# Residual kept by tokens; output and down projections with activations stationary and 512 weight columns moving

## The chip, the cores and the metric

The kernel runs on one core of one Trainium2 chip. The metric is the device time of one execution in microseconds; the figure given for a kernel is the median of several runs. Inputs are fp32 in HBM, and the output is fp32.

## What is computed

One layer on 256 tokens of width 2048. With `rmsnorm(u, w) = u * rsqrt(mean(u*u) + EPS) * w`, the reference is, cut to what matters:

```
h = rmsnorm(x, mix_norm_w);  u = h @ w_in                      # 2048 -> 5664
y_fox = fox_attention(...);  y_ssd = ssd_mixer(...)            # from slices of u
x = x + concat([y_fox, y_ssd]) @ w_out                         # 2048 x 2048
h = rmsnorm(x, ffn_norm_w)
g, up = split(h @ w_gate_up);  g = causal_dwconv(g, ...)       # 2048 -> 2 x 5632
x = x + (silu(g) * up) @ w_down                                # 5632 x 2048
h = rmsnorm(x, ple_norm_w)
x = x + sigmoid(h @ w_ple_gate) * (p @ w_ple_proj)
return rmsnorm(x, final_norm_w)
```

## The kernel before, in words

Every product is made of three TensorE products of rounded parts: a value is split into a high part (`hi`, type fp32r) and the rest (`lo`), and hi·hi, hi·lo and lo·hi are summed in PSUM. Weights stream from HBM in chunks of 256 rows by 512 columns (512 KB) through a ring of four slots: SyncE issues the load (`load_chunk`, two issues a chunk in the FFN), ScalarE makes `w_hi` (`make_hi`, L312), VectorE makes `w_lo` (`make_lo`, L317), and TensorE multiplies. ScalarE may make the high part of chunk n+4 only when TensorE is done with chunk n. All engines walk the chunks in the same order, and their other work is hung between chunks by hand: a step that belongs to the end of a group of chunks stands on ScalarE and VectorE `LEAD` = 3 chunks behind that end, since these engines run ahead of TensorE by that much. `plan()` fills the tables of such steps for the first part of the program.

The stages, in order: 11 groups of 8 chunks of `w_in` with the attention and the SSD part between them; `w_out` (4 groups `o0` to `o3` of 8 chunks); the FFN (22 units of 8 chunks, in a loop of two units); the down projection (4 groups of 22 chunks, partly in a loop on TensorE); the tail (per-layer gate `pg0` to `pg3`, 8 chunks each, with one chunk `pp0` to `pp3` of the projection of p after the sixth); the final norm and eight stores.

There are three forms of the product of one chunk, all with 6144 moving columns in sum:

- `multiply` (L332 to L334): a 128x128 tile of weights is stationary and 256 tokens move; 24 matmuls a chunk. Used in `w_in` (but for v) and in `w_out`.
- `multiply_wide` (L344, L346): a tile of weights is stationary; the high and low part of the activations, 512 columns, move past `w_hi`, and 256 columns past `w_lo`; 16 matmuls a chunk. Used in the FFN and the down projection.
- by tokens (L372 to L374, in `multiply_group`): a 128x128 tile of activations is stationary and 512 weight columns move; 12 matmuls a chunk. Used for v and in the tail.

The first two leave results with channels on partitions, the third with tokens on partitions. The residual is `xT`, with channels on partitions. It is made at the start by turning x (`turn_x`, L679) and copying each pair of turned tiles out of PSUM on VectorE (`copy_x`, L1538). After each group of `w_out` VectorE adds the result to it (`add_to_residual`, L1250; for the down projection `add_down`, L1262, four adds a group), ScalarE and VectorE make the parts of the next h from it (`make_h`, L969 and L1243), and GpSimd sums its squares (L646 to L653). `stats` on TensorE sums these over partitions (L713 before the second FFN unit, L716 in the tail). In the tail TensorE turns the residual back, eight 128x128 tiles for each of four groups (`turn_residual`, L936), and ScalarE copies it to `out_tok`. The last group of the tail has its weights kept (`last_hi`, `last_lo`), so that the first 128 tokens can be finished before the others.

## Time and profile before

| | |
|---|---|
| median of 3 runs | 1260.08 us (1260.00 to 1260.17) |
| the profiled execution | 1260.43 us, its span in the trace 1258.7 us |
| mean granted TensorE clock, share of full speed | 0.998 |
| TensorE busy | 1245.7 us, 99% of the span |
| VectorE, ScalarE, GpSimd busy | 856.7, 616.9, 60.8 us |
| HBM read | 224.03 MB, 180 GB/s over the span |

The profiled execution is 0.35 us longer than the median. A matmul's row in the trace starts when it is issued and overlaps the next one, so what one costs is the distance between starts, not its duration. A few per cent of the matmul rows are missing from the trace, so distances are read over stretches where every row is there, or over whole stages with the count that the program gives.

### The profile page before, as it was taken

The numbers are of one execution on the slowest core, as the hardware profiler recorded it, in microseconds if no ns is written. First come the engines' busy times: TensorE is split into PE (matmuls) and PEld (weight loads), VectorE is DVE, ScalarE is ACT, GpSimd is POOL, SyncE is SP. The second block draws the span as 40 slices with busy tenths as digits, with TensorE's granted clock in tenths as the row PEclk, the third lists the DMA queues.
The fourth block names the chain that finished last, engine by engine and source line by source line (L and its number), as shares of the span: only waits on it lengthen the run. The fifth ranks groups of instructions, "written<-read, shape, count | busy, mean of one in ns | idle before, by whom it ended". The sixth has DMA issues, their size and how long they took to land.

```text
span 1258.7 us, 21432 instructions
## 1 busy us (share of the span) xinstructions
PE 1245.7 (99%) x7838; PEld 1108.7 (88%) x7838; DVE 856.7 (68%) x1120; ACT 616.9 (49%) x810; POOL 60.8 (5%) x66
## 2 busy tenths in 40 slices
PE   8999999999999999999999999999999999999997
PEld 7999998789999888888888888888888888888885
DVE  6698777677678776767767677676746464646554
ACT  6544555656444454444444454454444344444555
POOL 2000000001213100000000000000001010101000
PEclk9999999999999999999999999999999999999999
DMA  8566555344656666666666666666665656566652
GB/s 256 168 183 184 157 146 155 114 114 125 199 172 203 186 193 186 185 196 183 191 193 185 194 187 187 194 187 188 191 190 166 216 160 217 164 212 202 198 185 101
DMA packets 165885, 226.94 MB, mean 180 GB/s; under 512 B 10209, under 2 KB 101381, under 8 KB 165701
## 3 DMA queue, kind: packets, MB, share of 16 engines
q1 hardware_dynamic: 165732, 225.90, 59.3%
q8 instruction: 38, 0.62, 0.2%
q0 software_dynamic: 96, 0.26, 0.1%
q14 instruction: 19, 0.15, 0.0%
HBM read 224.03 MB, written 2.10 MB: 180 GB/s over the span
## 4 chain that ended last, share of the span: by engine, by line
PE 97%; DVE 1%; DMA 1%; ACT 0%; SPq 0%; issue 0%; ACTq 0%; DVEq 0%
PE ps L344 39%; PE ps L346 19%; PE ps L332 8%; PE ps L333 8%; PE ps L334 8%; PE ps L372 4%; PE ps L374 4%; PE ps L373 3%; DMA w_raw<-in_w_in 1%; PE ps L764 1%; PE ps L767 1%; PE ps L808 1%; DVE h_parts L1243 0%; PE ps L791 0%; PE ps L821 0%; PE ps L778 0%
## 5 line engine op out<-in xcount | busy, mean ns | idle before, releaser
L317 DVE TENSOR_TENSOR w_lo<-w_raw,w_hi 128x1024 fp32r<-128x1024 f32 x413 | 505.9, 1230 | 318.2 <-ACT w_hi L312 317.5
L312 ACT ACTIVATE w_hi<-w_raw 128x1024 fp32r<-128x1024 f32 x413 | 435.9, 1059 | 459.4 <-PE ps L346 341.2
L344 PE MATMUL ps<-h_parts,w_hi 128*128 128x512 f32 x1408 | 488.6, 394 | 0.0
L346 PE MATMUL ps<-h_parts,w_lo 128*128 128x256 f32 x1408 | 390.2, 277 | 0.0
L344 PEld LDWEIGHTS ps<-h_parts,w_hi 128*128 128x128 f32 x1408 | 264.0, 188 | 61.5
L346 PEld LDWEIGHTS ps<-h_parts,w_lo 128*128 128x128 f32 x1408 | 264.2, 188 | 0.0
L344 PE MATMUL ps<-act_parts,w_hi 128*128 (+1 forms) x704 | 244.4, 392 | 0.0
L346 PE MATMUL ps<-act_parts,w_lo 128*128 (+1 forms) x704 | 196.8, 280 | 0.0
L332 PE MATMUL ps<-h_parts,w_hi 128*128 128x256 f32 x576 | 165.8, 288 | 0.6 <-DVE w_lo L317 0.6
L333 PE MATMUL ps<-h_parts,w_hi 128*128 128x256 f32 x576 | 162.9, 283 | 0.0
L334 PE MATMUL ps<-h_parts,w_lo 128*128 128x256 f32 x576 | 162.9, 283 | 0.0
L344 PEld LDWEIGHTS ps<-act_parts,w_hi 128*128 128x128 f32 x704 | 132.1, 188 | 29.5 <-issue 0.4
L346 PEld LDWEIGHTS ps<-act_parts,w_lo 128*128 128x128 f32 x704 | 132.2, 188 | 0.0
L332 PEld LDWEIGHTS ps<-h_parts,w_hi 128*128 128x128 f32 x576 | 110.2, 191 | 1.4 <-issue 1.3
L333 PEld LDWEIGHTS ps<-h_parts,w_hi 128*128 128x128 f32 x576 | 110.4, 192 | 0.0
L334 PEld LDWEIGHTS ps<-h_parts,w_lo 128*128 128x128 f32 x576 | 110.2, 191 | 0.0
L332 PE MATMUL ps<-mixHi,w_hi 128*128 128x256 f32 x256 | 71.8, 280 | 0.0
L334 PE MATMUL ps<-mixHi,w_lo 128*128 128x256 f32 x256 | 71.6, 280 | 0.0
L333 PE MATMUL ps<-mixLo,w_hi 128*128 128x256 f32 x256 | 71.6, 280 | 0.0
L372 PE MATMUL ps<-w_hi,h_parts 128*128 128x512 f32 x168 | 67.0, 399 | 0.6 <-DVE w_lo L317 0.6
L374 PE MATMUL ps<-w_hi,h_parts 128*128 128x512 f32 x168 | 65.8, 392 | 0.0
L373 PE MATMUL ps<-w_lo,h_parts 128*128 128x512 f32 x168 | 65.4, 389 | 0.0
(248 smaller groups left out, 1115.3 us busy)
## 6 DMA issues: line engine op xcount, KB each, us to landing
w_raw<-in_w_gate_up SPq DMA_DIRECT2D x352, 256.0 KB, 3.2
w_raw<-in_w_in SPq DMA_DIRECT2D x88, 512.0 KB, 3.7
w_raw<-in_w_down SPq DMA_DIRECT2D x88, 512.0 KB, 4.6
w_raw<-in_w_out SPq DMA_DIRECT2D x32, 512.0 KB, 4.6
w_raw<-in_w_ple_gate SPq DMA_DIRECT2D x32, 512.0 KB, 4.6
w_raw<-in_w_ple_proj SPq DMA_DIRECT2D x4, 512.0 KB, 5.3
out_x<-out_tok SPq DMA_DIRECT2D x8, 256.0 KB, 2.9
xtok<-in_x SPq DMA_DIRECT2D x3, 512.0 KB, 9.1
```

The lines of the kernel that those rows point to most:

```text
L312: act.activation(parts(n)[0], w_raw[:, n % RING, :], ACT.Copy).then_inc(w_hi_made, 1)
L317: dve.tensor_tensor(lo, w_raw[:, n % RING, :], hi, ALU.subtract).then_inc(w_lo_made, 1)
L332: pe.matmul(dst, hi, opHi(k), start=start and m % 2 == 0, stop=False, skip_group_check=True)
L333: pe.matmul(dst, hi, opLo(k), start=False, stop=False, skip_group_check=True)
L334: mm = pe.matmul(dst, lo, opHi(k), start=False, stop=stop, skip_group_check=True)
L344: pe.matmul(ps[:, bank_of[m], :], hi, both.rearrange("p b t -> p (b t)"), start=first and k == 0, stop=False, skip_group_check=True)
L346: mm = pe.matmul(ps[:, bank_of[m], T:2 * T], lo, both[:, 0, :], start=False, stop=last and k == 1, skip_group_check=True)
L372: pe.matmul(dst, a, hi, start=first and kk == 0, stop=False)
L373: pe.matmul(dst, a, lo, start=False, stop=False)
L374: mm = pe.matmul(dst, b, hi, start=False, stop=last and kk == 1)
L764: pe.matmul(ps[:, bank, 0:3 * P], sel[0:both, j:j + 1].to_broadcast([both, P]), row[:, :], start=start, stop=False, skip_group_check=True)
L767: mm = pe.matmul(ps[:, bank, dst:dst + P], ident_bf[:, :], mask[:, :], start=False, stop=True, skip_group_check=True)
```

## The change

- The residual is `xtok`, tokens on partitions, for the whole kernel: x as it is loaded. `xT`, `copy_x`, `turn_residual`, `copy_residual` and `out_tok` are gone; the tail adds into `xtok` and the stores read it.
- `w_out` and the down projection use the third form. The down projection is written out on TensorE, without a loop; each group has banks of its own.
- After each of the eight groups VectorE adds two [128x512] results to `xtok` (`add_columns`), ScalarE squares these columns and sums along them (`square_columns`), and TensorE, two chunks after the group's end, turns the new columns (`turn_columns`, eight 128x128 tiles) into the group's own PSUM banks. ScalarE and VectorE make the parts of h from PSUM, five chunks after the group's end in their own order.
- The sums of squares are summed over groups on VectorE (`sum_columns`), ScalarE takes the root, and VectorE inverts it (`invert_root`). For the FFN, `spread_rms` turns the column into rows on TensorE, as was done for the first norm only, and VectorE copies it. GpSimd no longer sums the residual's squares.
- At the start, h is made from the turned tiles in PSUM, without a copy between.
- The arena in SBUF starts at a multiple of 64 bytes instead of 32. It holds `act_parts`, `mixHi`, `mixLo`, `last_hi` and `last_lo`; before, these started at 32 past such a multiple. `w_hi`, `w_lo` and `h_parts` lie outside it and start at a multiple of 64 in both.

```
+    OUT_SETS, DOWN_SETS = (SET_B, SET_A, SET_C, SET_D), (SET_C, SET_A, SET_B, SET_D)
+    out_groups = [Group(f"o{i}", wout_v, COLS * i, "mix", b, KP, by_token=True) for i, b in enumerate(OUT_SETS)]
...
-        xT = sb("xT", [P, KD, T])
+        xtok = sb("xtok", [P, TT, D])
...
-        arena = (nc.sbuf_base + 31) // 32 * 32
+        arena = (nc.sbuf_base + 63) // 64 * 64
...
-        evacuated |= {f"o{i}": (x_new, NORM + 2 * i + 2) for i in range(NDN)}
-        evacuated |= {f"dn{i}": (x_new, 2 * NORM + 2 * i + 2) for i in range(NDN)}
+        evacuated |= {f"o{i}": (h_lo_made, KD + MT * (i + 1)) for i in range(NDN)}
+        evacuated |= {f"dn{i}": (h_lo_made, 2 * KD + MT * (i + 1)) for i in range(NDN)}
...
+        TURN_AFTER = 2
...
                 after(act_after, end[g] + LEAD, "leave_out", i)
                 after(dve_after, end[g] + LEAD, "leave_out", i)
+                all_after(end[g] + TURN_AFTER, "turn_out", i)
...
+            def turn_columns(i, banks, new):
+
+                pe.wait_ge(x_new, new)
+                for m in range(MT):
+                    for t in range(TT):
+                        k = MT * i + m
+                        mm = pe.transpose(ps[:, banks[m // 2], m % 2 * T + t * P:m % 2 * T + (t + 1) * P],
+                                          xtok[:, t, k * P:(k + 1) * P], ident[:, :])
+                mm.then_inc(x_turned, 1)
...
+                    if j == 0 and k == TURN_AFTER - 1:
+                        turn_out(NDN - 1)
+                    if j == 0 and k == SPREAD1_AT:
                         pe.wait_ge(*evacuated["o0"])
-                        stats(1, 4, columns=False)
+                        spread_rms(1, OUT_SETS[0][0])
...
+                        dst = ps[:, DOWN_SETS[g][t], :]
+                        pe.matmul(dst, a, hi, start=first and kk == 0, stop=False)
+                        pe.matmul(dst, a, lo, start=False, stop=False)
+                        mm = pe.matmul(dst, b, hi, start=False, stop=last and kk == 1)
...
+                    chunk(j)
+                    if g > 0 and j == TURN_AFTER - 1:
+                        turn_down(g - 1)
...
-                if n == STATS2_AT:
-                    stats(2, GATE_BANKS[1][0], rows_=False)
-                if n % GROUP == XTURN_AT:
-                    turn_residual(i)
+                if n == TURN_AFTER - 1:
+                    turn_down(NDN - 1)
...
+            def square_columns(norm, i):
+                for t in range(TT):
+                    done_ = TT + NDN * TT * (norm - 1) + TT * i + t
+                    act.wait_ge(x_new, NDN * TT * (norm - 1) + TT * i + t + 1)
+                    act.wait_ge(x_squared, done_)
+                    act.activation(sq[:, :, :], xtok[:, t, i * COLS:(i + 1) * COLS], ACT.Square,
+                                   accum_out=x_ssq[:, norm - 1, t, i:i + 1]).then_inc(x_squared, 1)
...
-                dve.wait_ge(h_hi_made, norm * KD + k + 1)
-                dve.scalar_tensor_tensor(hLo[:, k, :], xT[:, k, :], gain[:, k:k + 1], hHi[:, k, :],
+                dve.wait_ge(h_hi_made, norm * KD + k // 2 * 2 + 2)
+                dve.scalar_tensor_tensor(hLo[:, k, :], turned_x(norm, k)[0], gain[:, k:k + 1], hHi[:, k, :],
...
+            def add_columns(i, banks):
+
+                for t in range(TT):
+                    cols = xtok[:, t, i * COLS:(i + 1) * COLS]
+                    dve.tensor_tensor(cols, ps[:, banks[t], :], cols, ALU.add).then_inc(x_new, 1)
```

On TensorE, the start of the down projection before: a weight tile is stationary (the second name), 512 and 256 columns of `act_parts` move in turn.

```order
L344 MATMUL ps<-act_parts,w_hi 128x512 [waits w_lo_made,ffn_lo,ffn_out]
L346 MATMUL ps<-act_parts,w_lo 128x256
L344 MATMUL ps<-act_parts,w_hi 128x512
L346 MATMUL ps<-act_parts,w_lo 128x256
L344 MATMUL ps<-act_parts,w_hi 128x512
L346 MATMUL ps<-act_parts,w_lo 128x256
```

The same engine after the change, at the end of the second chunk of the second group of the down projection, with the new turn of the first group's columns:

```order
L916 MATMUL ps<-w_lo,act_parts 128x512
L917 MATMUL ps<-w_hi,act_parts 128x512
L718 MATMUL ps<-ident,xtok 128x128 [waits x_new]
L718 MATMUL ps<-ident,xtok 128x128 x7
L915 MATMUL ps<-w_hi,act_parts 128x512 [waits w_lo_made]
L916 MATMUL ps<-w_lo,act_parts 128x512
L917 MATMUL ps<-w_hi,act_parts 128x512
```

Weights now move, 512 columns at a time, and eight turns stand behind a wait for VectorE's adds. On VectorE, the start of the tail before (the first row is the low parts of chunks 0 to 3):

```order
L317 TENSOR_TENSOR w_lo<-w_raw,w_hi 128x1024 [waits w_hi_made] x4
L1262 TENSOR_TENSOR xT<-ps,xT 128x512 [waits w_used]
L1262 TENSOR_TENSOR xT<-ps,xT 128x512
L1262 TENSOR_TENSOR xT<-ps,xT 128x512 [waits x_part] x2
L1243 SCALAR_TENSOR_TENSOR h_parts<-xT,par,h_parts 128x256 [waits h_hi_made] x4
L317 TENSOR_TENSOR w_lo<-w_raw,w_hi 128x1024 [waits w_hi_made] x6
```

And after the change, at the same place:

```order
L318 TENSOR_TENSOR w_lo<-w_raw,w_hi 128x1024 [waits w_hi_made] x4
L1251 TENSOR_TENSOR xtok<-ps,xtok 128x512 [waits w_used]
L1251 TENSOR_TENSOR xtok<-ps,xtok 128x512
L318 TENSOR_TENSOR w_lo<-w_raw,w_hi 128x1024 [waits w_hi_made]
L1255 TENSOR_REDUCE x_sum<-x_ssq 128x2 [waits x_squared]
L1259 RECIPROCAL rms_col<-root 128x2 [waits root_made]
L318 TENSOR_TENSOR w_lo<-w_raw,w_hi 128x1024 [waits w_hi_made]
L1244 SCALAR_TENSOR_TENSOR h_parts<-ps,par,h_parts 128x256 [waits h_hi_made] x4
```

The adds are two instead of four, and the four instructions that make h stand two chunks later, with two low parts between.

## Rows read from the trace of the kernel before

**Rows 1.** The page: busy time of each engine, the granted clock, the chain.

```profile
PE 1245.7 (99%) x7838; PEld 1108.7 (88%) x7838; DVE 856.7 (68%) x1120; ACT 616.9 (49%) x810; POOL 60.8 (5%) x66
...
PEclk9999999999999999999999999999999999999999
...
PE 97%; DVE 1%; DMA 1%; ACT 0%; SPq 0%; issue 0%; ACTq 0%; DVEq 0%
```

**Rows 2.** TensorE in time (start, duration, instruction): first and last of 105 in `w_out`.

```profile
349.75 0.28 PE L332 MATMUL ps<-mixHi,w_hi 128*128 128x256 f32 x1
...
361.95 0.28 PE L334 MATMUL ps<-mixHi,w_lo 128*128 128x256 f32 x1
```

**Rows 3.** TensorE in time: the first matmul of the down projection and the first after it.

```profile
901.21 0.39 PE L344 MATMUL ps<-act_parts,w_hi 128*128 128x512 f32 x1
...
1145.55 0.40 PE L372 MATMUL ps<-w_hi,h_parts 128*128 128x512 f32 x1
```

**Rows 4.** TensorE in time: ends of a run of 11 by tokens in v, of 107 in the tail.

```profile
196.54 0.39 PE L373 MATMUL ps<-w_lo,h_parts 128*128 128x512 f32 x1
...
198.84 0.39 PE L374 MATMUL ps<-w_hi,h_parts 128*128 128x512 f32 x1
...
1189.81 0.39 PE L373 MATMUL ps<-w_lo,pHi 128*128 128x512 f32 x1
...
1213.93 0.40 PE L374 MATMUL ps<-w_hi,h_parts 128*128 128x512 f32 x1
```

**Rows 5.** TensorE in time: first and last of 36 with the kept weights.

```profile
1238.15 0.40 PE L372 MATMUL ps<-last_hi,h_parts 128*128 128x512 f32 x1
...
1246.34 0.40 PE L374 MATMUL ps<-last_hi,h_parts 128*128 128x512 f32 x1
```

**Rows 6.** TensorE in time: the first turn of the tail, and the small sums.

```profile
1162.75 1.03 PE L936 MATMUL ps<-ident,xT 128*128 128x128 f32 x8
...
1163.85 0.40 PE L373 MATMUL ps<-w_lo,pHi 128*128 128x512 f32 x1
...
1169.16 0.50 PE L716 MATMUL ps<-ones,sumsq 128*128 128x1 f32 x4
...
1169.84 0.39 PE L373 MATMUL ps<-w_lo,h_parts 128*128 128x512 f32 x1
```

**Rows 7.** TensorE in time: the sum before the FFN's second unit, and the first norm's spread.

```profile
426.54 0.59 PE L713 MATMUL ps<-sumsq,ones 128*128 128x256 f32 x2
...
427.20 0.28 PE L346 MATMUL ps<-h_parts,w_lo 128*128 128x256 f32 x1
...
43.03 0.61 PE L725 MATMUL ps<-ident,rms_col 128*128 128x128 f32 x4
...
43.60 0.28 PE L333 MATMUL ps<-h_parts,w_hi 128*128 128x256 f32 x1
```

**Rows 8.** TensorE in time: before the fifth chunk of the tail.

```profile
1156.26 0.39 PE L374 MATMUL ps<-w_hi,h_parts 128*128 128x512 f32 x1
1157.21 0.47 PE L372 MATMUL ps<-w_hi,h_parts 128*128 128x512 f32 x1 [0.57 <-DVE w_lo L317]
1157.52 0.40 PE L373 MATMUL ps<-w_lo,h_parts 128*128 128x512 f32 x1
```

**Rows 9.** VectorE in time, from the end of the down projection.

```profile
1148.05 2.48 DVE L1262 TENSOR_TENSOR xT<-ps,xT 128x512 f32<-128x512 f32 x4
1150.50 4.88 DVE L1243 SCALAR_TENSOR_TENSOR h_parts<-xT,par,h_parts 128x256 fp32r<-128x256 f32 x4
1155.31 5.16 DVE L317 TENSOR_TENSOR w_lo<-w_raw,w_hi 128x1024 fp32r<-128x1024 f32 x4
```

**Rows 10.** The start: VectorE's first copy, TensorE's second turn and first product.

```profile
5.38 0.69 DVE L1538 COPY xT<-ps 128x512 f32<-128x512 f32 x1 [1.79 <-PE ps L679]
...
7.53 0.66 PE L679 MATMUL ps<-ident,xtok 128*128 128x128 f32 x4 [0.98 <-DMA xtok<-in_x]
...
9.44 0.36 PE L332 MATMUL ps<-h_parts,w_hi 128*128 128x256 f32 x1 [0.16 <-DVE w_lo L317]
```

More of the change, by code:

```diff
@@ L354, in build, with turned_x @@
         WIDE_BANKS = ((0, 1, 2, 3), (4, 5, 6, 7))
+        def turned_x(norm, k):
+            if norm == 0:
+                bank, turn = X_BANKS[(k // 2) % len(X_BANKS)], k // 2
+            else:
+                bank = (OUT_SETS, DOWN_SETS)[norm - 1][k // MT][k % MT // 2]
+                turn = KD // 2 + NDN * (norm - 1) + k // MT
+            return ps[:, bank, k % 2 * T:(k % 2 + 1) * T], turn + 1
         def multiply_group(pe, n, g, c, only=(0, 1), between=None):
@@ L650, in _ @@
+            pool.wait_ge(a_exp, 1)
+            select(fdc[:, 3:4], fdc[:, 3:4], ALU.is_ge, 1.0, -H, 1, 0, 1).then_inc(a_ready, 1)
+            for b in range(WT // 2):
+                pool.wait_ge(gated, b // 2 + 1)
+                pair = xsT[:, 2 * b:2 * b + 2, :]
+                if b > 0:
+                    linked()
+                link(pool.tensor_tensor(sq[:, :, :] if b > 0 else sumsq[:, :, :], pair, pair, ALU.mult))
+                if b > 0:
                     linked()
                     link(pool.tensor_tensor(sumsq[:, :, :], sumsq[:, :, :], sq[:, :, :], ALU.add))
-                linked()
@@ L903, in _ @@
                 n0 = n_down + g * KDN
-                def chunk(j, q, first=False, last=False):
-                    at_ = (lambda k: act_parts[:, 2 * j + k, :, :]) if isinstance(q, int) else \
-                        (lambda k: act_parts[:, bass.ds(q * (2 * RING) + (2 * j + k), 1), :, :].rearrange("p a b t -> p (a b) t"))
-                    return multiply_wide(pe, n0 + j, at_, WIDE_BANKS[g % 2], first, last, q)
-                if g < 2:
-                    pe.wait_ge(ffn_out, NU + g)
-                else:
-                    pe.wait_ge(*evacuated[f"dn{g - 2}"])
@@ L940, in _ @@
+                if g < 3:
+                    pe.wait_ge(ffn_out, NU + g // 2)
+                pe.wait_ge(ffn_lo, NU - 2 if g == 0 else NU)
+                for j in range(KDN):
+                    if g == 0 and j == KDN - RING:
+                        pe.wait_ge(ffn_lo, NU)
+                    chunk(j)
+                    if g > 0 and j == TURN_AFTER - 1:
+                        turn_down(g - 1)
             for n, (g, c) in enumerate(tail):
@@ L1173, in _ @@
                     elif c == LEAD:
-                        for k in range(MT * (g - 1), MT * g):
-                            make_h(2, k, par_ple)
+                        leave_down(g - 1)
+                    elif c == LEAD + TURN_AFTER:
+                        turn_down(g - 1)
                 with act.Fori(0, (KDN - peeled) // RING) as q:
@@ L1190, in ple_sigmoid @@
                                    scale=rms_col[:, t:t + 1]).then_inc(ple_sig, 1)
-            def copy_residual(i):
-                for t in range(TT):
-                    act.wait_ge(xtok_turned, TT * i + t + 1)
-                    copy(out_tok[:, t, i * COLS:(i + 1) * COLS], ps[:, XTOK_BANKS[t], :]).then_inc(xtok_copied, 1)
             def square(i, t):
@@ L1525, in leave_out, with turn_out, leave_down, turn_down @@
                 dve.wait_ge(w_used, done[f"o{i}"] + 1)
-                add_to_residual(1, i, out_groups[i].banks)
+                add_columns(i, OUT_SETS[i])
+            def turn_out(i):
                 for k in range(MT * i, MT * (i + 1)):
                     make_h(1, k, par_ffn)
+            def leave_down(g):
+                dve.wait_ge(w_used, n_down + (g + 1) * KDN)
+                add_columns(g, DOWN_SETS[g])
+            def turn_down(g):
+                for k in range(MT * g, MT * (g + 1)):
+                    make_h(2, k, par_ple)
             def turn_par():
```

264 lines of the change are left out of this document (102 added, 162 removed).

## The prediction

> **What bounds the kernel now.** I read the page first: TensorE is busy for 99% of the span, the chain that ended last runs 97% through it, and its granted clock is in every slice 0.9 or more of full speed, in the mean 0.998, so at the 2.4 GHz level [rows 1]. VectorE is busy 68% and ScalarE 49% [rows 1]. So the time is a sum of TensorE's work, and the reader should look for three things: how far apart the starts of two matmuls lie in each form, how many turns there are, and at which few places TensorE still waits. For that I read TensorE in order of time, in stretches in which every row is there.
>
> The distance between starts, per 512 moving columns, is this. In `w_out`, 105 matmuls of 256 columns start from 349.75 to 361.95: 104 steps in 12.20 us, 0.1173 us each, 0.2346 us per 512 columns [rows 2]. The down projection takes 1145.55 - 901.21 = 244.34 us for 88 chunks of 6144 columns, 1056 times 512: 0.2314 us [rows 3]. By tokens, with 512 weight columns moving, the tail shows 24.12 us in 106 steps, 0.2275 us, and the v groups 2.30 us in 10, 0.230 us [rows 4]. The same form with the kept weights `last_hi` and `last_lo` moving takes 8.19 us in 35 steps, 0.2340 us [rows 5].
>
> **The change part by part.**
>
> Output projection. 32 chunks of 12 x 512 columns are 384 steps of 512. Before, 384 x 0.2346 = 90.1 us. After, the form is that of the tail, with the same ring of weights moving; only the stationary tiles come from another buffer. The trace bounds the pace at 0.2275 below and at 0.2340 above. I take 0.228: the tail's value is from 106 steps and v's from 10 that stand beside SSD work, so the tail is the nearer row. Gain: 384 x (0.2346 - 0.228) = 2.5 us.
>
> Down projection. 1056 x 0.228 = 240.8 us against 244.3: gain 3.6 us. The column count is the same, and no loop is left on TensorE; `w_out` is written out already and its matmuls start 0.117 us apart [rows 2], half the distance that is wanted here, so I cost the missing loop at nothing.
>
> Turns. Eight turns of eight tiles come in, four go out. The first one of the tail costs 1163.85 - 1162.75 = 1.10 us up to the second matmul behind it, of which 0.23 us is the matmul between: 0.87 us [rows 6]. Four more: +3.5 us. All of it is on the path, since TensorE has no idle time to put it in. A turn of the new kind differs in its buffers only; I know no row that would make it cheaper or dearer, and keep 0.8 to 1.0 us as its bounds.
>
> Small sums. The tail's sum over partitions, 1169.84 - 1169.16 = 0.68 us less one matmul of 0.23, goes: -0.45 us [rows 6]. The one before the second FFN unit (0.66 - 0.23 = 0.43 us) is replaced by a spread like that of the first norm (0.57 - 0.12 = 0.45 us): nothing [rows 7].
>
> The wait in the tail. At the fifth chunk TensorE is 1157.52 - 1156.26 = 1.26 us over two steps of 0.23: 0.80 us lost, 0.57 of it shown as a wait for `w_lo` [rows 8]. The cause stands on VectorE: four adds (2.48 us) and four parts of h (4.88 us) in one piece before the next low part, which begins at 1155.31 [rows 9]. After the change two adds (1.24 us) stand there, and the parts of h two chunks later. The next low part then can be ready long before 1156.5, so the 0.80 us go. What is late next? VectorE's adds end at 1148.05 + 1.24 = 1149.3. ScalarE's two squares, which no row shows at this place, are bounded by the dearest row of half that size, 1.22 us each [rows 9]: 1151.7. The high and the low part of chunk 4 at 1.29 us each, the low part's distance [rows 9]: 1154.3. TensorE wants it after four chunks and a turn, at 1145.55 + 4 x 2.74 + 0.87 = 1157.4. Nothing waits.
>
> The new wait. Each turn waits for the two adds, and all of TensorE's stream is queued behind it. TensorE gets there two chunks after the group's end, 1145.55 + 5.47 = 1151.0 in the tail's case; the adds end at 1149.3 [rows 3, 9]. The margin is 1.7 us, so I cost the eight waits at nothing.
>
> The kept weights. They start at 32 bytes past a multiple of 64 in SBUF, as does all of the arena, and are the only moving weights that do; they are also the only ones at 0.2340 [rows 5]. If that is the reason, 84 steps (36 for each half of the tokens and 12 of p) fall to 0.228: -0.5 us. The bounds are 0 and 0.55. I take 0.5, since same form and same stationary buffer leave little else.
>
> The start. The copy of 0.69 us goes from the chain to the first product [rows 10]. But TensorE itself gets its second turn only at 7.53, when x has landed, and runs filler until shortly before 9.44, where it waits only 0.16 us for the low part [rows 10]. Gain 0.2 us; the ends are 0 and 0.7.
>
> The squares that GpSimd did, the 16 copies and the rest on ScalarE and VectorE cost nothing: both engines have a third of the span free or more and run ahead of TensorE by up to four chunks.
>
> The sum: -2.5 - 3.6 + 3.5 - 0.45 - 0.8 - 0.5 - 0.2 = -4.6 us. It is made against the profiled execution, 1260.43 us, of which 1258.7 is the span: 1255.85. The median of the runs is 0.35 lower, so I predict 1255.5 us.
>
> One rule is to be weighed here. What the rows show is that 512 columns cost 14 ns more than 512 cycles at 2.4 GHz (213.3 ns), and 256 columns 10.6 ns more than theirs [rows 2, 4]. The Trainium skill, "TensorE: Matmul & The Clock Gate", section "Back-to-back issue gap", gives N / 2.4 + 2.5 ns. By it the new form would save only 12 x 2.5 ns on each of 32 chunks and 4 x 2.5 ns on each of 88, together 1.8 us instead of 6.1, and the time would be near 1259.8. The trace does not agree with the 2.5 ns in any form.
>
> **The rivals.**
>
> The pace belongs to the stage, not to the form. In the tail VectorE and ScalarE do less than beside v, where the same form runs at 0.230 [rows 4]. If `w_out` and the down projection run at 0.230, the gains shrink by 1440 x 0.002 = 2.9 us: 1258.4 us. For it: the v rows. Against it: those are 10 steps against 106, and neither `w_out` nor the down projection has matmuls of another kind in between, as v has. The page's rule would end close to this case.
>
> Slower: the new pair of operands is as slow as the kept weights, 0.2340, for instance because stationary and moving buffers disturb each other in a way that the tail's pair does not. Then `w_out` gains 0.2 us, the down projection loses 1056 x 0.2340 - 244.3 = 2.8 us, nothing comes from the kept weights, and the turns are not paid for: -0.2 + 2.8 + 3.5 - 0.45 - 0.8 - 0.2 = +4.6, so 1264.7 us. The point from which the change loses is a pace of (334.4 - 1.5) / 1440 = 0.2312 us, where 334.4 is the two stages now and 1.5 the sum of the other terms. Against it: both runs of by-token rows with the ring's weights are below that.
>
> Slower by waits: the adds come over 1.7 us later than I reckon, because VectorE is behind when a group ends. At 1 us lost in each of eight turns: 1263.5 us. Against it: VectorE's idle third.
>
> **How the numbers follow.** The forecast has 0.71, with a range of its own of 1254.0 to 1257.5 (paces of 0.2275 to 0.2293, the start's 0.7). The slower-stage case has 0.18, the pace of 0.2340 0.06, the waits 0.03; 0.02 are left for a larger gain. A measurement of this kernel can tell 0.2%, 2.5 us, from no change. So: faster 0.73, within 0.2% 0.18, slower 0.09. The range takes in the forecast and the first rival: 1252.8 to 1260.2 us.
>
> **What would show it.** In the trace of the changed kernel: steps of 0.228 us in both projections, the down projection in 240 to 241 us without its turns and `w_out` 2.5 us shorter; eight turns of 0.87 us with no idle time before them; no wait in the first chunks of the tail; the kept weights at 0.228; the first product at 9.3. The prediction is wrong if the steps are at 0.230 or more, if the turns wait, or if a low part is late after a group's end. TensorE's busy share stays at 99% in every case.

## The result, and the profile after

The changed kernel takes 1262.26 us, the median of 20 runs (1261.83 to 1262.71). The kernel before took 1260.01 us beside it (20 runs, 1259.77 to 1262.66). The ratio is 1.0016, with a 95% interval from 1.0009 to 1.0023. So the change costs some 2 us, where a gain of 4.6 was forecast; the time lies outside the range. The profiled execution took 1262.27 us, and its span is 1260.5 us, 1.8 us more than before.

The page of the changed kernel, in the same lines as [rows 1]:

```profile
PE 1248.1 (99%) x7132; PEld 1081.4 (86%) x7132; DVE 821.5 (65%) x1107; ACT 622.0 (49%) x834; POOL 23.2 (2%) x34
...
PEclk9999999999999999999999999999999999999999
...
PE 98%; DMA 1%; SPq 0%; ACT 0%; issue 0%; DVE 0%; ACTq 0%; DVEq 0%
```

TensorE issues 706 matmuls fewer than before and is busy 2.4 us longer. Its clock is as high as before. The groups of instructions of the page show where (line, engine, operation, tiles, shapes, count; then busy time and mean ns of one). First before, then after:

```profile
L344 PE MATMUL ps<-h_parts,w_hi 128*128 128x512 f32 x1408 | 488.6, 394 | 0.0
L346 PE MATMUL ps<-h_parts,w_lo 128*128 128x256 f32 x1408 | 390.2, 277 | 0.0
```

```profile
L345 PE MATMUL ps<-h_parts,w_hi 128*128 128x512 f32 x1408 | 497.6, 399 | 0.0
L347 PE MATMUL ps<-h_parts,w_lo 128*128 128x256 f32 x1408 | 395.4, 281 | 0.0
```

These are the FFN's matmuls. The change left them alone: the same instructions, the same number, the same buffers. Their busy times are up by 9.0 and 5.2 us (the rows of the two groups overlap in time, so the two numbers don't add up). To see what each stage did, I take the distance from the first matmul of a stage to the first of the next, in us. The front is from the first product to the output projection, and the tail is to the last matmul.

| | first product at | front | output | FFN | down | tail | span |
|---|---|---|---|---|---|---|---|
| before | 9.44 | 312.42 | 90.55 | 488.80 | 244.34 | 103.54 | 1258.7 |
| after | 8.82 | 311.86 | 90.27 | 498.65 | 242.11 | 99.21 | 1260.5 |
| difference | -0.62 | -0.56 | -0.28 | +9.85 | -2.23 | -4.33 | +1.8 |

Outside the FFN the stages lost 8.0 us together, three turns more in the output projection and three in the down projection already paid. The FFN, which the prediction costed at one turn, takes 9.85 us more. When the FFN became slow is seen in TensorE in time (start, duration, instruction, count), around its second unit:

```profile
416.59 1.03 PE L718 MATMUL ps<-ident,xtok 128*128 128x128 f32 x8
417.38 0.48 PE L345 MATMUL ps<-h_parts,w_hi 128*128 128x512 f32 x1
417.70 0.28 PE L347 MATMUL ps<-h_parts,w_lo 128*128 128x256 f32 x1
...
425.68 0.28 PE L347 MATMUL ps<-h_parts,w_lo 128*128 128x256 f32 x1
425.79 0.61 PE L704 MATMUL ps<-ident,rms_col 128*128 128x128 f32 x4
426.16 0.48 PE L345 MATMUL ps<-h_parts,w_hi 128*128 128x512 f32 x1
426.47 0.28 PE L347 MATMUL ps<-h_parts,w_lo 128*128 128x256 f32 x1
```

From 417.70 to 425.68 lie 46 steps of a half pair: 7.98 / 23 = 0.347 us for a pair (a matmul of 512 and one of 256 columns), 832 cycles at 2.4 GHz. Then come the small matmuls of `spread_rms`: two of 128 columns, which stand as x4, since a matmul of plain fp32 operands leaves two rows in the trace. Behind them a pair costs more, here between 599.72 and 619.86, 57 pairs in 20.14 us:

```profile
599.72 0.40 PE L345 MATMUL ps<-h_parts,w_hi 128*128 128x512 f32 x1
...
619.86 0.40 PE L345 MATMUL ps<-h_parts,w_hi 128*128 128x512 f32 x1
```

That is 0.3533 us, 848 cycles. It stays so up to 909.48: 2734 recorded steps at 424.0 cycles each. Nothing waits meanwhile. The kernel before shows both paces too. In its first FFN unit 29 pairs take 10.24 us, 0.3531 each; after its small matmul (L713, at 426.54 in [rows 7]) 59 pairs take 20.46 us, 0.3468 each:

```profile
415.93 0.40 PE L344 MATMUL ps<-h_parts,w_hi 128*128 128x512 f32 x1
...
426.17 0.40 PE L344 MATMUL ps<-h_parts,w_hi 128*128 128x512 f32 x1
...
599.26 0.40 PE L344 MATMUL ps<-h_parts,w_hi 128*128 128x512 f32 x1
...
619.72 0.39 PE L344 MATMUL ps<-h_parts,w_hi 128*128 128x512 f32 x1
```

So the same stream of matmuls runs at one of two paces, and it changes from one to the other at a few small matmuls. The kernel before runs 40 of its 1408 pairs at the slow pace, the changed one 16 and then 1368. The 1344 pairs more, at 16 cycles each, are 9.0 us.

### The profile page after: what moved, and what is told of

Read it like the earlier page. It is cut to its first block, busy times and chain, and to the rows that moved or that the text cites. A ratio compares the mean times of both kernels' runs of the same rounds, so it can differ in the third digit from the quotient of the medians.

```text
span 1260.5 us, 19756 instructions
## 1 busy us (share of the span) xinstructions
PE 1248.1 (99%) x7132; PEld 1081.4 (86%) x7132; DVE 821.5 (65%) x1107; ACT 622.0 (49%) x834; POOL 23.2 (2%) x34
## 4 chain that ended last, share of the span: by engine, by line
PE 98%; DMA 1%; SPq 0%; ACT 0%; issue 0%; DVE 0%; ACTq 0%; DVEq 0%
PE ps L345 26%; PE ps L347 13%; PE ps L916 6%; PE ps L915 6%; PE ps L917 6%; PE ps L382 6%; PE ps L384 6%; PE ps L383 6%; PE ps L333 5%; PE ps L335 5%; PE ps L334 5%; PE ps L763 1%; DMA w_raw<-in_w_in 1%; PE ps L718 1%; PE ps L766 1%; PE ps L807 1%
## 5 line engine op out<-in xcount | busy, mean ns | idle before, releaser
L345 PE MATMUL ps<-h_parts,w_hi 128*128 128x512 f32 x1408 | 497.6, 399 | 0.0
L915 PE MATMUL ps<-w_hi,act_parts 128*128 128x512 f32 x352 | 137.2, 390 | 0.0
L917 PE MATMUL ps<-w_hi,act_parts 128*128 128x512 f32 x352 | 137.0, 389 | 0.0
L916 PE MATMUL ps<-w_lo,act_parts 128*128 128x512 f32 x352 | 136.9, 389 | 0.0
L917 PEld LDWEIGHTS ps<-w_hi,act_parts 128*128 128x128 f32 x352 | 66.1, 188 | 13.8
L915 PEld LDWEIGHTS ps<-w_hi,act_parts 128*128 128x128 f32 x352 | 66.1, 188 | 13.7
L916 PEld LDWEIGHTS ps<-w_lo,act_parts 128*128 128x128 f32 x352 | 66.1, 188 | 13.6
L382 PE MATMUL ps<-w_hi,mixHi 128*128 128x512 f32 x128 | 50.3, 393 | 0.0
```

What stands on the lines that cost most here:

```text
L345: pe.matmul(ps[:, bank_of[m], :], hi, both.rearrange("p b t -> p (b t)"), start=first and k == 0, stop=False, skip_group_check=True)
L382: pe.matmul(dst, a, hi, start=first and kk == 0, stop=False)
L915: pe.matmul(dst, a, hi, start=first and kk == 0, stop=False)
L916: pe.matmul(dst, a, lo, start=False, stop=False)
L917: mm = pe.matmul(dst, b, hi, start=False, stop=last and kk == 1)
```

## The experiments

### What the small matmuls decide

The first four kernels put two theories against each other. One: every interruption by small matmuls toggles the pace. The other: what stands in the interruption decides, and the sum of before (one matmul of 256 columns) sets it fast while the spread (two of 128) leaves it slow. In each of them the work added has no use for the result.

`e1_joined`, from the kernel after: one more matmul of 256 columns of plain fp32 right behind the spread.

```
                         spread_rms(1, OUT_SETS[0][0])
+                        pe.matmul(ps[:, OUT_SETS[0][1], 0:T], ones[:, :], xtok[:, 0, 0:T], ...)
```

> The changed kernel with one more fp32 matmul of 256 columns right behind the spread in the first FFN unit, in the same block of small matmuls. In the changed kernel two starts of a pair (512 and 256 columns) are 0.3467 us apart before the spread and 0.3533 us after it, to the end of the FFN. Theory 'every block of fp32 matmuls between the rounded ones switches the pace': still one block, so the pace stays at 0.3533 and the time near 1262.4 us. Rival 'the last or the wider of the small matmuls sets it' (the kernel before has a 256-column one there and runs at 0.3467 behind it): 0.3467 and 1253.3 us. Rival 'nothing at this place matters, the pace comes from where the buffers lie': 0.3533, 1262.4.

It takes 1253.72 us against 1259.95 of before: 0.9947 (0.9925 to 0.997). A matmul more, and 8.5 us less than the kernel after. Its FFN takes 489.96 us, and the page's first group of the FFN has the numbers of before, 488.6 us and 394 ns. TensorE in time:

```profile
425.89 0.61 PE L704 MATMUL ps<-ident,rms_col 128*128 128x128 f32 x4
426.34 0.60 PE L894 MATMUL ps<-xtok,ones 128*128 128x256 f32 x2
426.58 0.58 PE L345 MATMUL ps<-h_parts,w_hi 128*128 128x512 f32 x1
```

`e2_apart`, from after: the same matmul in an interruption of its own, a chunk later.

```
+                    if j == 0 and k == SPREAD1_AT + 1:
+                        pe.matmul(ps[:, OUT_SETS[0][1], 0:T], ones[:, :], xtok[:, 0, 0:T], ...)
```

> The same added matmul, one chunk later, so that it is a block of its own. Theory 'every block switches the pace': a second switch brings back 0.3467 for the rest of the FFN, 9.1 us less and 0.4 us more for the matmul: 1253.6 us. Rival 'the last small matmul sets it': the same 0.3467. Rival 'where the buffers lie': 0.3533, 1262.7 us.

1253.91 us, 0.9953 (0.9934 to 0.9973). Between the spread and the new matmul a pair takes 848 cycles, behind it 832: the pace changes at this one instruction.

`e3_double`, from before: its sum twice in a row.

```
-                    mm = pe.matmul(ps[:, bank, 0:T], ones[:, :], sumsq[:, 0, :], ...)
+                    for _ in range(2):
+                        mm = pe.matmul(ps[:, bank, 0:T], ones[:, :], sumsq[:, 0, :], ...)
```

> The kernel before with its sum over partitions in the first FFN unit issued twice in the same block. Theory 'every block switches': one block as before, so the FFN stays at 0.3467 and the time is 1260.3 us. Rival 'the number of small matmuls decides' (one gives the fast pace, two of the spread the slow one): 0.3533 in the FFN and, since nothing switches it back, in the down projection too, 14 us more: 1274 us.

1260.31 us, 1.0004 (0.9993 to 1.0015); the FFN takes 489.23 us, fast.

`e4_halves`, from before: its sum as two matmuls of 128 columns.

```
-                    mm = pe.matmul(ps[:, bank, 0:T], ones[:, :], sumsq[:, 0, :], ...)
+                    for c in range(TT):
+                        mm = pe.matmul(ps[:, bank, c * P:(c + 1) * P], ones[:, :], sumsq[:, 0, c * P:(c + 1) * P], ...)
```

> The kernel before with that sum made as two matmuls of 128 columns instead of one of 256, as many and as wide as those of the changed kernel's spread. Theory 'every block switches': 0.3467, 1260.1 us. Rivals 'the number decides' and 'the width decides': 0.3533 in the FFN and in the down projection, 1274 us. Rival 'where the buffers lie': 0.3467, 1260.1 us.

1269.13 us, 1.0073 (1.0044 to 1.0103): the old kernel, with the same sum in two halves, is 9.2 us slower. It is the loss of the change, made in the kernel before and by one line. Its FFN takes 497.94 us, and 57 pairs from 599.73 on take 20.14 us, as in the kernel after.

The expectation had 5 us more, since it let the down projection become slow too. It did not: 244.36 us, as before. That miss is the first sign that the down projection, the same form with another moving buffer, is not touched at the place where that buffer lies in this kernel.

`e5_turned`, from after: one 128x128 turn behind the spread.

```
                         spread_rms(1, OUT_SETS[0][0])
+                        pe.transpose(ps[:, OUT_SETS[0][1], 0:P], xtok[:, 0, 0:P], ident[:, :])
```

> The changed kernel with one 128x128 turn (fp32 transpose) right behind the spread, in the same block. The eight turns of the changed kernel bring the pair to 0.3467 us, a block that ends in fp32 matmuls of 128 columns leaves or brings it to 0.3533, one that ends in a matmul of 256 columns brings 0.3467. Theory 'the last small instruction of a block sets the pace, and a turn is a fast one': 0.3467, time 1253.6 us. Rival 'the whole block's length or make-up sets it' : can stay at 0.3533, 1262.4 us.

1254.39 us, 0.9955 (0.9935 to 0.9975), fast: a third small matmul of 128 columns does it as well.

`e9_ahead`, from after: the matmul of 256 columns ahead of the spread.

```
+                        pe.matmul(ps[:, OUT_SETS[0][1], 0:T], ones[:, :], xtok[:, 0, 0:T], ...)
                         spread_rms(1, OUT_SETS[0][0])
```

> The changed kernel with the added fp32 matmul of 256 columns ahead of the spread, not behind it: the same instructions in the block as in the joined variant, in the other order. Theory 'the last small instruction decides': the block ends in a matmul of 128 columns, so the FFN stays at 0.3533 us a pair and the time is 1262.7 us. Rival 'the length or make-up of the block decides': as the joined variant, 0.3467 and 1253.7 us.

1253.88 us, 0.995 (0.993 to 0.997), fast. So it isn't the last small matmul that decides, but the interruption as a whole. Toggling falls by `e1_joined`, fast behind its second interruption, and by `e4_halves`, slow behind its first.

`e10_onewide`, from `e1_joined`: the spread itself as a single matmul of 256 columns. VectorE multiplies `ident` by the column, 128 columns for each half of the tokens; the stationary operand is `ones`.

```
+                        pe.wait_ge(diag_made, 2)
+                        pe.matmul(ps[:, OUT_SETS[0][0], 0:T], ones[:, :], sumsq[:, 0, :], ...)
...
+                            for t in range(TT):
+                                dve.tensor_scalar(sumsq[:, 0, t * P:(t + 1) * P], ident[:, :], rms_col[:, t:t + 1], None, ALU.mult)
```

> The changed kernel with its spread made as one fp32 matmul of 256 columns (VectorE multiplies the identity with each half's column, ones are stationary) instead of two of 128. By 'the last small instruction decides' and by 'its width decides' the FFN runs at 0.3467 with nothing added on TensorE: 1253.3 us, 6.7 us under the kernel before. By 'only the number of instructions or chance decides' it may stay at 1262.3 us.

1253.02 us, 0.9944 (0.9928 to 0.9961). It needs no instruction without a use. The spread and the FFN in time, 58 pairs in 20.11 us, 0.3467 each:

```profile
425.54 0.59 PE L895 MATMUL ps<-sumsq,ones 128*128 128x256 f32 x2
...
599.65 0.40 PE L346 MATMUL ps<-h_parts,w_hi 128*128 128x512 f32 x1
...
619.76 0.40 PE L346 MATMUL ps<-h_parts,w_hi 128*128 128x512 f32 x1
```

### What the places in SBUF decide

The change also moved the arena: `act_parts` started at 32 past a multiple of 128 bytes before (128800), and on such a multiple after (128896). The ring and `h_parts` start on one in both. That it is a multiple of 128 after is chance: the line asks for one of 64, and the small buffers ahead of the arena had grown by 96 bytes. In the kernel before the same line gives 128832, 64 past a multiple of 128.

`e7_arena`, from before: the arena on a multiple of 64, which puts `act_parts` at 64 past a multiple of 128.

```
-        arena = (nc.sbuf_base + 31) // 32 * 32
+        arena = (nc.sbuf_base + 63) // 64 * 64
```

> The kernel before with its arena on a multiple of 64 bytes, as the changed kernel has it, and nothing else changed. Theory 'the start of the moving buffer decides': the kept weights fall from 0.2340 to 0.228 a matmul (-0.5 us), while w_out's matmuls of 256 columns, which now move from a buffer on a multiple of 64, rise from 0.1173 to 0.120 (768 of them: +2 us) : 1261.5 us. Rival 'the form and the stage decide': no change, 1260.0 us.

1263.17 us, 1.0029 (1.0017 to 1.004). The output projection is 90.27 us, 0.28 less, where 2 us more were expected. The down projection, wide as before, became slow, 248.73 us; 56 pairs take 19.79 us, 0.3534 each. The kept weights, which were to fall to 0.228 us, did not: 35 steps take 8.16 us, 0.2331 each or 560 cycles, on a multiple of 64 now. First the down projection, then the kept weights:

```profile
999.86 0.40 PE L344 MATMUL ps<-act_parts,w_hi 128*128 x1
...
1019.65 0.40 PE L344 MATMUL ps<-act_parts,w_hi 128*128 128x512 f32 x1
...
1240.53 0.39 PE L372 MATMUL ps<-last_hi,h_parts 128*128 128x512 f32 x1
...
1248.69 0.39 PE L374 MATMUL ps<-last_hi,h_parts 128*128 128x512 f32 x1
```

Two more things stand in this trace. The output projection has two paces of its own: 272 cycles a matmul (58 steps from 330.03 to 336.60), and 283 (166 steps from 337.38 to 356.93). Between the two lies a small fp32 matmul of 256 columns:

```profile
336.71 0.59 PE L852 MATMUL ps<-sumsq,ones 128*128 128x256 f32 x2
```

And the FFN is fast from its first unit on (832 cycles a pair from 412.03 to 424.16), ahead of any small matmul, though its own operands lie where they lay in the kernel before, whose first unit is slow. Only the arena's place differs, which these matmuls don't read, so it points to what ran before them.

`e8_arena32`, from `e1_joined`: the arena 32 bytes further, so that `act_parts` and the mixer's parts are at 32 as in the kernel before. One line.

```
-        arena = (nc.sbuf_base + 63) // 64 * 64
+        arena = (nc.sbuf_base + 63) // 64 * 64 + 32
```

> The changed kernel with the added matmul of 256 columns behind the spread (fast FFN), and with its arena at 32 bytes past a multiple of 64, as it was before the change. Theory 'the start of the moving buffer decides': both projections keep 0.2267 a matmul, since there the arena holds only the stationary tiles; the kept weights go back to 0.234, +0.5 us: 1254.2 us. Rival 'the stationary buffer's place counts too': the projections get slower, 0.230 would be +5 us.

1264.03 us, 1.0028 (1.0015 to 1.0042), 10.3 us more than `e1_joined`, of which the down projection is 6.9 and the output projection 2.4. The theory that only the moving buffer's place counts falls: in these stages the ring moves, and it stands where it stood; the stationary tiles moved. The same 20 us in both kernels, first the kernel after (89 steps in 20.18 us, 0.2267 us), then this one (87 in 20.30, 0.2333):

```profile
999.61 0.39 PE L915 MATMUL ps<-w_hi,act_parts 128*128 128x512 f32 x1
...
1019.79 0.39 PE L917 MATMUL ps<-w_hi,act_parts 128*128 128x512 f32 x1
```

```profile
999.68 0.40 PE L918 MATMUL ps<-w_hi,act_parts 128*128 128x512 f32 x1
...
1019.98 0.40 PE L918 MATMUL ps<-w_hi,act_parts 128*128 128x512 f32 x1
```

So the change of form alone, with the places of before, gains 0.6 us in the output projection (92.63 less three turns of 0.88 against 90.55) and loses 2.0 in the down projection (249.02 less three turns against 244.34). Of the change's gains in these two stages, 2.4 of 2.9 us and the whole 4.9 come from the place of the arena.

`e6_shifted`, from after: `h_parts` at 32 and the ring at 64 past a multiple of 128, by moving two small buffers ahead of them.

```
+        rms_col = sb("rms_col", [P, TT])
         h_parts = sb("h_parts", [P, KD, 2, T], F32R)
+        x_sum = sb("x_sum", [P, 3, TT])
```

> The changed kernel, nothing added, but h_parts starts 32 bytes past a multiple of 64 instead of on it (two small tensors are moved beside it; the ring of weights and the arena stay where they are relative to 64 bytes). Theory 'only a moving buffer on a multiple of 64 knows the slow pace' (in the kernel before act_parts starts at 32 past one and runs at 0.3467 whatever the FFN did; mixHi too, 0.1173 a matmul of 256 where h_parts has 0.120): the FFN runs at 0.3467 with the spread as it is, and the matmuls of w_in come nearer to 0.1173: 1253 us from the FFN alone, down to 1248 with w_in. Rival 'the place in SBUF has no part in it': 1262.3 us, 0.3533 in the FFN.

1266.19 us, 1.0049 (1.0026 to 1.0071), a clear miss: both theories had less. The FFN is slow throughout (848 cycles a pair), behind the eight turns too, the down projection takes 549 cycles a matmul instead of 544 (244.39 us), and the tail 560.

`m1_places` is a program of its own that computes no layer and passes x through: TensorE alone runs the three forms over constant data, with stationary and moving buffers at 0, 32, 64 and 96 past a multiple of 128, and then the FFN's form behind fourteen kinds of interruption.

> No layer at all, x is only passed through: TensorE runs each of the three forms on constant data with the stationary buffer and the moving buffer starting at 0, 32, 64 and 96 bytes past a multiple of 128, 16 pairs of places a form, each behind an fp32 matmul of 256 columns; then the FFN's form again behind two of 128 columns, and behind fourteen kinds of small block at place 0, 0. Theory 'the pair of places sets the pace': by tokens 544 cycles of 2.4 GHz a matmul (0.2267 us) at 0, 0; 549 with the moving one at 64; 560 with either at 32; the FFN's form 832 a pair at stationary 0 and moving 32 whatever the block, 848 at moving 64, and 832 or 848 at 0, 0 by the block. Rival 'other engines' traffic sets the pace': with TensorE alone all places give the same.

Cycles at 2.4 GHz from start to start; the rows of the table are the place of the stationary operand, its columns that of the moving one. The forms by tokens and narrow are given for one matmul, over the last 24 steps of each field; the wide form for a pair of 512 and 256 columns, behind one fp32 matmul of 256 columns and, in the second run of its fields, behind two of 128:

| stationary at | by tokens: 0, 32, 64, 96 | wide, behind one of 256: 0, 32, 64, 96 | wide, behind two of 128 | narrow: 0, 32, 64, 96 |
|---|---|---|---|---|
| 0 | 545, 560, 549, 560 | 832, 832, 848, 840 | 848, 832, 837, 840 | 288, 280, 283, 288 |
| 32 | 560, 544, 560, 549 | 849, 832, 832, 847 | 849, 848, 833, 848 | 284, 288, 283, 283 |
| 64 | 560, 560, 544, 560 | 848, 832, 832, 832 | 848, 847, 848, 832 | 272, 284, 288, 283 |
| 96 | 563, 560, 560, 544 | 832, 848, 847, 832 | 832, 848, 847, 832 | 282, 272, 284, 288 |

What counts is how the two places stand to each other. By tokens, equal places cost least, and 32 apart costs 16 cycles more. Narrow, equal places cost most. In the wide form the moving operand 32 bytes further than the stationary one (96 and 0 is such a field too, modulo 128) is fast in every row and behind both kinds; of the other twelve fields, five were fast the first time and only one the second. The kernels agree, in cycles: the tail after, equal places, 544; the kept weights before, 0.2340 us = 562 [rows 5]; `e8_arena32`, 32 and 0, 560; `e6_shifted`, tail 32 and 64, 560, and down 0 and 64, 549; `e7_arena`, wide 0 and 64, 848 a pair.

Counted modulo 128 they don't all agree, though. The kept weights of `e7_arena` are at 0 and 64 and take 560 cycles, where the table and the down projection of `e6_shifted` have 549. The addresses tell the two apart modulo 256: in the table's field and in `e6_shifted` the moving buffer starts 64 bytes above the stationary one (192 and 128 past a multiple of 256 in the kernel), in `e7_arena` 64 below it (64 and 128), as in the table's field 64 and 0, which has 560. Likewise the kept weights of before lie 96 below `h_parts` (32 and 128); the field 96 and 0 has 563. So it is the distance modulo 256 that fits the by-token stages here. No run was made to test it, and the two paces of the output projection in `e7_arena` show that the distance alone doesn't fix the pace in every form.

The kinds of interruption, all at equal places, gave no rule: slow behind one matmul of 256 (848 cycles, though the table's first field, at the same places and behind the same kind, has 832) and fast behind two of 128, the reverse of the kernels.

`m2_again` is the same program with only the wide form, at the places 0 and 0 and at 0 and 32; each of four kinds of interruption comes six times in a row, with 32 pairs behind each. It computes no layer either.

> No layer at all, x is only passed through. The FFN's form on constant data at places 0, 0 and at stationary 0, moving 32, four chunks behind each small block, and each of four kinds of block six times in a row. Theory 'the kind of block decides at 0, 0': six equal paces for each kind. Rival 'the block shifts a phase that the stream before it left, whatever its kind': at 0, 0 paces of 832 and 848 cycles mixed within a kind. Both: 832 every time at 0, 32.

| cycles a pair behind | places 0 and 0 | places 0 and 32 |
|---|---|---|
| one of 256 columns | 832 (6 of 6; the program's first eight pairs, which are slower, left out) | 832 (6 of 6) |
| two of 128 | 833, 848, 833, 832, 847, 832 | 833 (6 of 6) |
| one turn | 832 (6 of 6) | 832 (6 of 6) |
| eight turns | 832 (6 of 6) | 832 (6 of 6) |

The same interruption, with the same instructions ahead of it, is followed by the slow pace two times in six. Here a slow and a fast one, in time:

```profile
99.71 0.61 PE L137 MATMUL ps<-plain 128*128 128x128 f32 x4
100.07 0.48 PE L98 MATMUL ps<-acts,hi 128*128 128x512 f32 x1
...
121.84 0.27 PE L98 MATMUL ps<-acts,lo 128*128 128x256 f32 x1
121.95 0.40 PE L98 MATMUL ps<-acts,hi 128*128 128x512 f32 x1
122.18 0.28 PE L98 MATMUL ps<-acts,lo 128*128 128x256 f32 x1
122.30 0.39 PE L98 MATMUL ps<-acts,hi 128*128 128x512 f32 x1
...
123.00 0.60 PE L137 MATMUL ps<-plain 128*128 128x128 f32 x4
123.36 0.48 PE L98 MATMUL ps<-acts,hi 128*128 128x512 f32 x1
```

The interruptions themselves look the same. The pairs behind the first come 848 cycles apart, those behind the second 832. What differs stands ahead of them. A fast stretch has one of two rhythms: ahead of the slow case the starts lie 230, 117, 230 and 116 ns apart, ahead of the fast one 232, 118, 231 and 112, seen above as 0.11 and 0.12 us from a 256 to the next 512. Of the six times, the two that were followed by the slow pace stand behind the first rhythm, two of the others behind the second and two behind the slow pace. The spread of the kernel after stands behind the first rhythm too. But `e4_halves`, whose halves stand behind the slow pace, stayed slow. So at equal places the kind of interruption isn't all, and the stream ahead has a part in it. With the moving operand 32 bytes further, all 24 are fast.

`e12_h32`, from `e10_onewide`, puts that to use: `h_parts` behind the ring, at 32 past a multiple of 128, while the ring stays at 0.

```
-        h_parts = sb("h_parts", [P, KD, 2, T], F32R)
         w_raw = sb("w_raw", [P, RING, CHUNK])
         w_hi, w_lo = ...
+        x_sum = sb("x_sum", [P, 3, TT])
+        h_parts = sb("h_parts", [P, KD, 2, T], F32R)
```

> The one-matmul variant (1253.0 us) with h_parts placed behind the ring of weights, 32 bytes past a multiple of 128, all else where it was. By the map of places: the FFN's form with its moving buffer 32 bytes past the stationary one's place runs at 832 cycles a pair whatever the block, so 0.3467 us stays; w_in's matmuls of 256 columns go from 288 and more cycles to 280-282, 1728 of them by 0.003 to 0.004 us, -5 to -7 us; the by-token matmuls in which h is stationary (192 in v, 432 in the tail) go from 544 to 560 cycles, +4.2 us. Sum 1250 to 1252.5 us. Rival 'the map of constant data on an otherwise idle core does not carry over': 1253.0, or slower.

1252.04 us, 0.9938 (0.9925 to 0.9952), the lowest time of all and within the 1250 to 1252.5 expected. Its interval overlaps that of `e10_onewide` (0.9928 to 0.9961), so how much it gains over that kernel isn't settled. In the first FFN unit, ahead of any small matmul, the pairs settle at 832 cycles, where `e10_onewide` has 847. The front is 308.76 us, 2.8 less than in `e10_onewide`, and the tail 101.48, 2.2 more. In `w_in` a narrow matmul takes 16.10 us / 138 = 0.1167 us, 280 cycles as in the table; in the kernel before it was 15.84 / 132 = 0.1200, 288. The rows of this kernel and of before:

```profile
49.86 0.28 PE L334 MATMUL ps<-h_parts,w_hi 128*128 128x256 f32 x1
...
65.96 0.28 PE L334 MATMUL ps<-h_parts,w_hi 128*128 128x256 f32 x1
```

```profile
50.10 0.28 PE L332 MATMUL ps<-h_parts,w_hi 128*128 128x256 f32 x1
...
65.94 0.28 PE L332 MATMUL ps<-h_parts,w_hi 128*128 128x256 f32 x1
```

The tail, by tokens with 32 apart, takes 560 cycles as foreseen (87 steps in 20.31 us).

The front was expected to gain 5 to 7 us. The 1728 narrow matmuls at 0.0033 us are 5.7, and v (192 by tokens, 15 cycles each) gives 1.2 back; 1.7 us of it didn't come. The front scatters by about 1 us from kernel to kernel (below), and where the rest is I haven't traced.

## Why the prediction was wrong

**The step that failed** is the one on the small sums: "is replaced by a spread like that of the first norm (0.57 - 0.12 = 0.45 us): nothing". The instructions themselves cost nothing more (from the last matmul ahead, 425.68, to the second behind, 426.47, it is 0.79 us, and 0.79 in the kernel before as well). What stands behind them cost 9 us, and the FFN as a whole was not in the sum but for its turn: +9.85 us, a turn of 0.88 and 9.0 of pace. `e4_halves` makes this loss alone in the kernel before, and `e1_joined`, `e5_turned`, `e9_ahead` and `e10_onewide` take it off the kernel after. The rivals had a pace for the new form and none for the old one in an untouched stage, so the range was too narrow on that side; the time came by neither of them.

It could have been seen that such a thing exists. The FFN of before changes its pace at L713, and I read its small matmuls there [rows 7] for their own price alone.

**The output projection**: -0.28 us with three turns in it (the fourth lies in the FFN), so -2.9 where -2.5 was written. The steps are 0.2267 us (89 in 20.18 us, from 339.77 on), a little below the 0.2275 that bounded them.

**The down projection**: -2.23 with three turns, so -4.9 where -3.6 was written; again 0.2267 instead of 0.228. Both gains came, somewhat larger than written, but the reason isn't right. I took the pace from the tail as one of the form. It is one of the form and the places: with the arena where it was, the same form takes 0.2333 us (`e8_arena32`), near the 0.2340 of the slower rival, and the change loses. That the two buffers came to lie alike was luck. That rival named the mechanism rightly ("stationary and moving buffers disturb each other in a way that the tail's pair does not"); the line on the arena kept it off. The first rival, that the pace belongs to the stage, did not come: both projections run at 0.2267. Yet v, in the form and at the places of the tail, starts 549 cycles apart on average in the kernel after as well; which of its paces a stage gets is open there too.

**The turns** cost 0.88 each, where 0.87 was written. The first stands above: 417.70 - 416.59 = 1.11, less 0.23. None waits. The wait list of TensorE in the kernel after (tile, line, what released it: us, times, longest) has only the start, and one low part there:

```profile
PE ps L670 <- DMA xtok<-in_x: 1.5, 1, 1.5
PE ps L652 <- DVE idle_in L1543: 1.3, 1, 1.3
PE ps L333 <- DVE w_lo L318: 0.3, 1, 0.3
```

**The tail**: -4.33 us. By the prediction's terms it loses three turns, since it had four and has one (-2.6), its sum over partitions (-0.45), the wait (-0.8) and the slower kept weights (-0.5): -4.4. The wait of [rows 8] is gone. The adds behind the last group are two, and h now is made when GpSimd is idle:

```profile
1154.21 1.28 DVE L1251 TENSOR_TENSOR xtok<-ps,xtok 128x512 f32<-128x512 f32 x2
...
1161.20 1.65 DVE L1244 SCALAR_TENSOR_TENSOR h_parts<-ps,par,h_parts 128x256 fp32r<-128x256 f32 x4
```

The kept weights are as fast as the ring's now, 35 steps in 7.93 us, 0.2266:

```profile
1240.27 0.39 PE L382 MATMUL ps<-last_hi,h_parts 128*128 128x512 f32 x1
...
1248.20 0.39 PE L384 MATMUL ps<-last_hi,h_parts 128*128 128x512 f32 x1
```

The place was named as their cause, and the runs bear it out, though not as "32 past a multiple of 64": in `e7_arena` they lie on a multiple of 64 and still take 0.2331. What counts is their distance from the place of `h_parts`, and that it became zero was luck.

**The start**: the first product is at 8.82 instead of 9.44, 0.6 us where 0.2 was written and 0.7 was the end. One trace says little here: in the other kernels with this start it comes at 8.75 to 9.98, in the middle at 9.13, and in those with the old one at 9.38 to 9.96, so some 0.3 us is what the runs support. The rows of the changed kernel:

```profile
7.93 1.24 PE L652 MATMUL ps<-idle_in 128*128 128x512 bf16 x5
8.82 0.47 PE L333 MATMUL ps<-h_parts,w_hi 128*128 128x256 f32 x1
```

The front came out 0.56 us shorter besides. It lies between 311.0 and 312.9 us in all kernels here that don't move `h_parts` or the ring, so I put that down to nothing.

The rule that the prediction weighed, "Back-to-back issue gap" in "TensorE: Matmul & The Clock Gate" of the Trainium skill, is N / 2.4 + 2.5 ns, given there for a matmul by itself. The fastest of the forms here takes 544 cycles for 512 columns, 32 and not 6 more, and the narrow one 272 to 288 for 256. No run here agrees with it, and no single number can stand in its place.

**What stays open.** At equal places, why one interruption leaves the slow pace and another the fast one. In the FFN of the layer's kernels with `h_parts` and the ring at 0 it went by the kind behind every interruption (slow: two of 128 columns; fast: anything with a 256 in it, or with one or eight turns), and no run of a kernel lies 9 us from the others of the same kernel. Without an interruption it was slow in all of them but `e7_arena`, and over constant data it did not go by the kind. And why the distance of 32 bytes is fast for one form and slow for another: that two streams of reads from SBUF meet there is a guess that no row shows.

## What to carry to other kernels

Measure the pace (start to start) in each stage, and look for places at which it changes inside one stage: a stage that an edit leaves alone may still change its pace when a small matmul ahead of it changes. Where nearly all the time is TensorE's, the start addresses of the stationary and the moving operand are a parameter to be tuned like any other: here one line that shifts an arena by 32 bytes was worth 10 us, twice what the whole change was expected to gain. Prefer a pair of places that was fast behind everything tried, as `e12_h32` does for the FFN; in the layer itself only its one spread of 256 columns and the eight turns were tried there.

## What the runs showed of the hardware

- With fp32r operands, what a matmul costs depends on how far apart its two operands start: 544 to 563 cycles for 512 columns, 272 to 288 for 256, 832 to 849 for a pair of both. Distances that are equal modulo 128 bytes can differ (by tokens 549 with the moving one 64 above, 560 with it 64 below).
- At equal places the pair has two steady paces, 832 and 848 cycles, and keeps one for hundreds of microseconds (from 426.47 to 909.48 in the kernel after). All changes seen in the FFN stand at small matmuls. Which pace follows isn't settled by the interruption's kind alone: in `m2_again` two of 128 columns gave the slow one 2 times in 6.
- The form by tokens has a second pace at equal places too, and no small matmul is needed to bring it. In the kernel after two matmuls start late, at 1231.84 and 1232.18. Behind them the starts lie 0.231 us (554 cycles) apart, 10 steps in 2.31 us. Twelve matmuls with `pHi` and `pLo` follow, which lie 64 bytes above the ring (modulo 256) and take 560 anyway, then six more steps of 0.232 with `h_parts`, and from 1239.13 on it is 0.2266 again:

```profile
1232.41 0.40 PE L384 MATMUL ps<-last_hi,h_parts 128*128 128x512 f32 x1
...
1234.72 0.40 PE L382 MATMUL ps<-last_hi,pHi 128*128 128x512 f32 x1
```

- VectorE makes four parts of h in 4.88 us while GpSimd sums squares [rows 9] and in 1.65 us with GpSimd idle, at the same shape (the source is SBUF in the one and PSUM in the other, so these rows don't tell the two reasons apart). The low parts, which have no PSUM in them, bear on this: in the kernel before, from 322 us on, four of the six beside GpSimd's work took 1.63 to 1.77 us, the other two 1.22 and 1.23, and none of the 323 others over 1.23.
